# Rotary embedding in a two-layer transformer block: the halves of each head exchanged by on-chip transfers in place of a matmul with a swap matrix

## The reference, cut to what matters

```
def apply_rope(x, cos, sin):
    x1, x2 = x[..., :half], x[..., half:]
    return jnp.concatenate([x1 * cos - x2 * sin, x2 * cos + x1 * sin], axis=-1)
```

## Time and profile before

| | |
|---|---|
| median of 3 runs | 1800.82 us (1797.72 to 1802.49) |
| the profiled execution, its own time | 1802.4 us |
| its span | 1800.6 us |
| mean granted PE clock | 0.978 |
| PE busy | 1684.6 us (94% of the span) |
| PEld busy | 1244.1 us (69%) |
| DVE, POOL, ACT busy | 968.5, 788.7, 661.8 us |

### The profile page before, as it was taken

The page is one execution under the profiler, slowest core; times in us unless marked ns, Lnnn a source line. Parts: engine busy times, 40 slices in busy tenths (PEclk is TensorE's granted clock), DMA queues, the critical chain, the costliest instruction groups (busy, mean ns, idle before and its releaser), DMA issues.

```text
span 1800.6 us, 27888 instructions
## 1 busy us (share of the span) xinstructions
PE 1684.6 (94%) x11035; PEld 1244.1 (69%) x11035; DVE 968.5 (54%) x1715; ACT 661.8 (37%) x1218; POOL 788.7 (44%) x575
## 2 busy tenths in 40 slices
PE   7999988977989999999999998997987999999998
PEld 3688877866856678666876787786776645745646
DVE  3544488895458841686428835456995612122112
ACT  3222267775243310243013113225875364053130
POOL 2244435562424553345413343543232657458463
PEclk9999999999999999999999999998999899999999
DMA  9344352322124423345226332533102324334332
GB/s 316 48 109 112 98 145 79 92 58 72 46 71 141 129 81 96 94 129 153 79 62 199 126 74 52 121 86 105 32 2 71 82 71 117 94 88 111 83 82 82
DMA packets 314352, 174.99 MB, mean 97 GB/s; under 512 B 87519, under 2 KB 309615, under 8 KB 314223
## 3 DMA queue, kind: packets, MB, share of 16 engines
q1 hardware_dynamic: 284686, 143.70, 30.5%
q10 hardware_dynamic: 29536, 29.51, 5.1%
HBM read 159.04 MB, written 2.83 MB: 90 GB/s over the span
## 4 chain that ended last, share of the span: by engine, by line
PE 59%; DVE 5%; POOL 3%; issue 2%; ACT 2%; DMA 1%; SPq 1%; DVEq 0%; ACTq 0%; POOLq 0%
PE acc L878 53%; POOL split_w L655 1%; PE small L1147 1%; DVE prob_t L1757 1%; DVE stat L1743 1%; DVE act L1579 1%; PE side L1061 1%; DVE o_sum L1769 1%; ACT prob_t L1380 1%; DVE scaled_ffn L1593 0%; POOL pair_w L755 0%; POOL split_w L652 0%; PE small L1076 0%; PE side L870 0%; PE acc L1044 0%
## 5 line engine op out<-in xcount | busy, mean ns | idle before, releaser
L878 PE MATMUL acc<-act,pair_w 128*128 128x512 f16 x3168 | 582.9, 345 | 8.2 <-DVE act L1579 7.8
L878 PEld LDWEIGHTS acc<-act,pair_w 128*128 128x128 f16 x3168 | 309.6, 99 | 268.4 <-issue 9.4
L878 PE MATMUL acc<-act,split_w 128*128 128x512 f32 (+1 forms) x1920 | 378.4, 355 | 9.6 <-DVE act L1579 4.6
L878 PEld LDWEIGHTS acc<-act,split_w 128*128 128x128 f32 x1920 | 307.5, 190 | 63.3 <-DVE act L1843 5.1
L652 POOL TENSOR_SCALAR split_w<-raw_w 128x1024 fp32r<-128x1024 f32 (+1 forms) x120 | 126.9, 1058 | 441.4 <-PE acc L878 335.7
L878 PE MATMUL acc<-hidden,split_w 128*128 128x512 f32 (+1 forms) x1584 | 308.9, 356 | 6.6 <-POOL split_w L655 3.6
L878 PEld LDWEIGHTS acc<-hidden,split_w 128*128 128x128 f32 x1584 | 260.9, 189 | 52.1 <-POOL split_w L655 5.3
L655 POOL TENSOR_TENSOR split_w<-raw_w,split_w 128x1024 fp32r<-128x1024 f32 (+1 forms) x120 | 281.4, 2345 | 10.0
L752 POOL TENSOR_SCALAR pair_raw<-pair_raw,weight_scale 128x1024 f32<-128x1024 f32 x88 | 106.4, 1209 | 356.1 <-ACT pair_w L1429 356.1
L1906 DVE SCALAR_TENSOR_TENSOR mod_acc<-mod_chunk,silu_c,mod_acc 128x256 f32<-128x256 f32 x280 | 224.4, 844 | 4.0
L1604 DVE SCALAR_TENSOR_TENSOR x_t<-acc,mod,x_t 128x512 f32<-128x512 f32 x96 | 60.4, 659 | 253.9 <-PE acc L878 253.4
(11 more groups left out here) (189 smaller groups left out, 1885.5 us busy)
## 6 DMA issues: line engine op xcount, KB each, us to landing
mod_chunk<-in_w_mod ACTq DMA_DIRECT2D x28, 1024.0 KB, 5.3
pair_raw<-in_w_gate SPq DMA_DIRECT2D x44, 512.0 KB, 4.1
pair_raw<-in_w_up SPq DMA_DIRECT2D x44, 512.0 KB, 5.4
raw_w<-in_w_in SPq DMA_DIRECT2D x64, 256.0 KB, 3.7
raw_w<-in_w_down SPq DMA_DIRECT2D x32, 512.0 KB, 4.2
raw_w<-in_w_mod SPq DMA_DIRECT2D x24, 512.0 KB, 4.1
mod_start<-in_w_mod SPq DMA_DIRECT2D x8, 1024.0 KB, 12.0
ks<-q_split SPq DMA_DIRECT2D x64, 96.0 KB, 2.2
```

The source lines that it names most:

```text
L878: mm = pe.matmul(acc[slot][:, a:b], weights[:, part == 2, k, :], moving[:, part == 1, k, a:b], start=(k == 0 and part == 0), stop=(k == n ...
```

## The change

The swap matrix, its load at the start and the swap matmul go. In its place ACT starts four transfers from SBUF to SBUF, each of 32 partitions by 512 floats (64 KB), which put q_n with its halves exchanged into q_sin. They stand in ACT's step j behind the copy and the square of unit j and ahead of `take_row(j-1)`. DVE waits for the four landings instead of for PE, and its multiply now reads q_sin (SBUF) where it read `small` (PSUM). Nothing else moves; lines of the changed program are numbered 1 to 12 lower.

```
-                def after_norm(j):
-                    if not 0 <= j < 16 or QKV[j][0] not in "qk":
-                        return
-                    i = l * N_ROPE + rope_before(j)
-                    pe.wait_ge(q_normed, l * N_QK + qk_before(j) + 1)
-                    if i >= 1:
-                        pe.wait_ge(q_sin_ready, i)
-                    pe.matmul(small[:, 0:LAT], swap[:, :], q_n[i % 2][:, :], start=True, stop=True).then_inc(q_swapped, 1)
...
-                    after_norm(j - 3)
                     after_copy(j - 1)
...
+                def swap_halves(j):
+                    if not 0 <= j < 16 or QKV[j][0] not in "qk":
+                        return
+                    r = l * N_ROPE + rope_before(j)
+                    sc.wait_ge(q_normed, l * N_QK + qk_before(j) + 1)
+                    if r:
+                        sc.wait_ge(q_ready, r)
+                    for p in range(0, P, 32):
+                        sc.dma_start(q_sin[p:p + 32, :], q_n[r % 2][p ^ 32:(p ^ 32) + 32, :]).then_inc(swap_in, 16)
...
                             sc.activation(sq[slot][:, 0:w], acc[slot][:, 0:w], ACT.Square).then_inc(q_sq, 1)
+                    swap_halves(j - 3)
                     take_row(j - 1)
                     round_high(j - 3)
...
-                    ve.wait_ge(q_swapped, r + 1)
-                    if r:
-                        ve.wait_ge(q_ready, r)
-                    ve.tensor_tensor(q_sin[:, :], small[:, 0:LAT], sin[:, :], ALU.mult).then_inc(q_sin_ready, 1)
+                    ve.wait_ge(swap_in, 64 * (r + 1))
+                    ve.tensor_tensor(q_sin[:, :], q_sin[:, :], sin[:, :], ALU.mult).then_inc(q_sin_ready, 1)
```

More of the change, by code:

```diff
@@ L206, in trunk @@
 def trunk(nc, x, c, ctx, c_ctx, w_mod, b_mod, norm_attn, norm_ffn, w_in, qk_norm, sink, rpb, w_out,
-          w_gate, w_up, w_down, k_ident, k_pairs, k_swap, k_cos, k_sin, k_window, k_columns, out):
+          w_gate, w_up, w_down, k_ident, k_pairs, k_cos, k_sin, k_window, k_columns, out):
     inv_dram = nc.dram_tensor("inv_rows", [2, 2, TOK], F32, kind="Internal").ap()
@@ L230, in trunk @@
         pair_ones = place("pair_ones", [P, P], F32)
-        swap = place("swap", [P, P], F32)
         ones = place("ones", [P, P], F32)
@@ L362, in trunk @@
         qkv_copied, q_sq, q_ssq, q_root, q_inv = sem("qkv_copied"), sem("q_sq"), sem("q_ssq"), sem("q_root"), sem("q_inv")
-        q_normed, q_swapped, q_cos_ready, q_sin_ready, q_ready = (
-            sem("q_normed"), sem("q_swapped"), sem("q_cos_ready"), sem("q_sin_ready"), sem("q_ready"))
+        q_normed, swap_in, q_cos_ready, q_sin_ready, q_ready = (
+            sem("q_normed"), sem("swap_in"), sem("q_cos_ready"), sem("q_sin_ready"), sem("q_ready"))
         v_ps, v_ready, v_hi = sem("v_ps"), sem("v_ready"), sem("v_hi")
@@ L470, in _ @@
             load_start(2)
-            for dst, src in ((pair_ones, k_pairs), (swap, k_swap), (cos, k_cos), (sin, k_sin)):
+            for dst, src in ((pair_ones, k_pairs), (cos, k_cos), (sin, k_sin)):
                 sp.dma_start(dst[:, :], src[:, :]).then_inc(consts_in, 16)
@@ L1943 @@
 N_VECS = 4 + 3 * DEPTH
-N_CONST = 7
+N_CONST = 6
 def shape_constants():
@@ L1952, in shape_constants @@
     pairs = (p[:, None] // 64 == p[None, :] // 64).astype(f)
-    swap = (p[:, None] == (p[None, :] ^ 32)).astype(f)
     t = np.arange(LAT)
@@ L1967, in shape_constants @@
         columns[:, VARIANT[cb]] = np.where(ok, 0, NEG)
-    return {"k_ident": ident, "k_pairs": pairs, "k_swap": swap, "k_cos": cos, "k_sin": sin.astype(f),
+    return {"k_ident": ident, "k_pairs": pairs, "k_cos": cos, "k_sin": sin.astype(f),
             "k_window": window, "k_columns": columns}
```

## The result

The changed kernel takes 1847.42 us in the median (1840.68 to 1854.52, 4 runs) against 1801.39 us before (4 runs beside it): 1.0257 times as long, 95% interval 1.0238 to 1.0276, 46 us more. The profiled execution is the slowest of the four: 1854.5 us, span 1852.7, so its rows show 52 us of loss against the 1802.4 us of the execution profiled before.

A forecast was written before the change was run, and what follows sets the result against it. PE, busy without a break in both projections, was taken as the bound. Waits less swaps +17.3 and clock +12.6 gave +29.9 us, so 1831 us against the median (chance 0.48), 8-in-10 range 1810 to 1853.

The forecast's parts named there:

- the second rival: Slow transfers: issues at 0.60 us, landings at 3.4 us, +1.6 at each of fourteen waits, +22: 1853 us; chance 0.14.
- (a): First issue on ACT's queue, behind the square's start: T + 2.35 us (T: end of a unit's matmuls on PE).
- (b): Three more issues on ACT's queue at 0.50 us each; the last starts at T + 3.85 us.
- (c): Landing of the exchange transfers taken as 2.1 us, so the data are there at T + 5.95 us.
- Swaps, -13.6: The 16 swap matmuls on PE's path in the projections go, 0.85 us each: -13.6 us.
- (d), (e): DVE multiplies from T + 6.0, add ends T + 7.45; reciprocal, then PE's transpose at T + 7.95: wait 2.4 us.
- the three named: Places where multiply and POOL pass may touch for half a us: behind unit 12, and unit 7 of the second layer.
- Unit 8 of the second layer: Longest transpose wait, about 5 us: ACT copies narrow unit 7 only at T + 3.2; +3.4 us net.
- Clock: Waits in PE's work lower its clock: nine of fourteen bring a spell losing 1.4 us, +12.6 us (bounds 0 and 20).
- the clock did not hold: Rival that the clock holds in the projections: everything as forecast without the slow spells, 1818 us; chance 0.17.
- the quick transfers: Rival: issues at 0.38 us, landings at 1.9, -8 us, and waits too short to lower the clock: 1810 us; chance 0.10.
- the faster case (1787): Rival: rotation chain ends before PE reaches its transpose, only the saved swap matmuls count: 1787 us; chance 0.04.

The follow-up runs named there:

- the best version: Changed kernel with DVE's rotation of unit m-4 moved behind the reciprocal of unit m-2: 1789.62 us, 0.993 of the kernel before.

## Why the prediction was right, and what was off

Direction and mechanism hold: PE unbroken before, broken after at ten transposes and by the values behind units 11 and 12, the wait held up by DVE's order. The undoing of that order and the delay without transfers show it; it is not only argued. The size was less good, and partly lucky. Measured were 46 us more against 30 forecast. The two projections lengthened by 22 + 27 = 49 us, one short of the 50 beyond which the forecast was to be called wrong. Both conditions of the second rival, issues at 0.6 us and landings over 3 us, came true at most exchanges, and its 1853 us is nearer to the result than my 1831; the range holds the result because that rival was its upper end. An issue that came earlier than I had it (a) hid part of the error in (b) and (c).

- Swaps, -13.6: the best version gains 11.5 us of it with 1.9 us of wait left.
- (a) Issue: too late by 0.8 us. The first transfer left at T + 1.56, even ahead of the copy's start (107.90 against 107.94), not behind the square's as the earlier trace rows had led me to say. (b) Issue 0.61 us, not 0.50, and one of the four here 1.30 us: last start T + 4.2 for 3.85.
- (c) Landing: the step that was mis-sized. I took the middle of the earlier trace rows, 2.1 us, where the end of an exchange is the latest of four transfers: 3.67 here, over 3 in 11 of 16. Where the slowest took 2.1 us (the exchange of unit 6 here, those of units 2, 6 and 7 and, in the second layer, 2 and 7 with the weight loads moved) the waits were 1.6 to 2.5 us, against 2.4 forecast; where it took 3.1 to 3.8 us they were 2.5 to 4.1. The exchange of unit 4 goes by something else: it landed after 2.4 and 2.0 us, and PE waited 3.3 and 6.2 us, because the copy ahead of it waited for the norm and the multiply met POOL (below). The second rival had the landing nearly right; what I held against it, that the middle value was taken beside such loads too, was no reason, because a median of single transfers doesn't bound the slowest of four.
- (d), (e) Multiply 0.69, add 0.69, reciprocal, transpose 0.29 us behind its start: as worked out (but 6.0 + 0.73 + 0.69 is 7.42, not 7.45). The multiply meets POOL for 0.5 us (1.17 to 1.28 us) at four places, the three named and behind unit 7 of the first layer.
- Unit 8 of the second layer: about 5 us of wait forecast, 6.2 measured; the copy of unit 7 waited for the norm until T + 4.0, not 3.2. Values: 1.5 + 1.6 = 3.1 us a layer forecast, 2.5 + 0.2 = 2.7 and 2.8 + 1.2 = 4.0 measured; the first wait was too small in the sum, the second too large.
- Waits less swaps: +17.3 forecast; 42.9 us idle less the 1.2 us of before less 13.6 = +28.1 in the profiled execution.
- Clock: +12.6 forecast, 9.6 + 11.3 = 20.9 measured there. The count was nearly right: nine spells (stretches at the lower clock) forecast, ten in the trace, eight of them behind the ten waiting transposes and two behind waits for values (210.97 and 1261.10). The size of one was not. Six last about 3.4 us, as forecast, but four about 7 us; the second line below is one of these. And the earlier trace rows was misread: its 18 matmuls were not all at the lower level, for the mean clock over their 5.70 us is 0.64 (first line; columns as in the earlier trace rows). At a clock of 0.50, 3.4 us cost 1.7 us and not 1.4.

```profile
1084.78:1090.48 5.70, 5.65 (x18) 4.06 (x18) 5.63 (x11) 2.41 (x5) 0.00 (x0) 0.64 0.00 0
190.50:197.50 7.00, 5.66 (x18) 4.86 (x19) 3.00 (x6) 1.00 (x2) 1.27 (x1) 0.51 0.25 59
```

Two transposes of the changed kernel, one without a spell and one with; the wait before them stands in brackets:

```profile
178.28 0.28 PE L977 MATMUL mod_ps<-ident,inv_tok 128*12 128x128 f32 x1 [1.74 <-DVE inv_tok L1643]
178.31 4.41 PE L877 MATMUL acc<-act,split_w 128*128 128x512 f32 x24
191.84 0.38 PE L977 MATMUL mod_ps<-ident,inv_tok 128*12 128x128 f32 x1 [3.61 <-DVE inv_tok L1643]
191.87 6.98 PE L877 MATMUL acc<-act,split_w 128*128 128x512 f32 x24
```

The same 24 matmuls take 4.41 us behind the short wait and 6.98 behind the long one. Some 3 us of the 52 lie outside the projections. The remaining rivals: the clock did not hold, the quick transfers did not come, and the faster case (1787) needed the chain out of PE's way, which a reordering does and the change alone does not.

## What to carry to other kernels

Before a short on-chip step is replaced by a transfer, look at what stands behind the waiting instruction in its engine's order: here a 0.23 us reciprocal, queued behind a rotation whose data came 6.8 us later after the unit's end (7.8 against 1.05), cost more than everything the change saved. Move what the bound engine needs ahead of the new wait first; with that done here, the transfers cost nothing measurable. Where several transfers make one result, take the slowest of them beside whatever else is on the queues, and let one transfer do it if it can. Whether one transfer can make this exchange as quickly was not tried; the run with one left the exchange out.

## What was not expected of the hardware

- One transfer of 256 KB (without the exchange) was in place 3.0 us after its issue started, beside four of 64 KB that took 6.3 us from the first issue (107.90 to 114.18).
- A transfer on ACT's queue can be issued before the compute instructions written ahead of it have begun (107.90; copy at 107.94, square at 108.64).
- The clock's loss doesn't go by the sum of the waits. With 39 us of idle PE the delayed kernel before (eight multiplies more) shows 0.97 and 0.94 in the projections, the changed one with 43 us 0.93 and 0.91. Behind a wait of 2.04 us the 24 matmuls took 5.98 us in the run with moved weight loads, behind one of 3.20 us 4.49 us in the delayed one. What decides stays open.
